# A hybrid decoder step on one core: wide state space tables, moved scans, value tiles and gate between the levels, the embedding's affine part on GpSimd

## The reference, cut to what matters

```python
x = layer_norm(concat(meta, prompt, sample), g_emb, b_emb)           # embedding norm
q, fpre, v, gate, u = split(x @ w_in + b_in)                         # five groups of 512
f = lb + (1 - lb) * sigmoid(fpre);  k = (1 - lb) * sigmoid(-fpre)
o, S = gated_linear_recurrence(q, k, v, f, S0)                       # 4 heads of 128 x 128
o_hg = o * rsqrt(mean(o * o)) * norm_g * silu(gate)
h[t] = a_bar * h[t-1] + B_bar @ u[t];  y = C @ h + d * u             # complex diagonal state space
z = gelu(y);  o_ssm = z * sigmoid(z @ w_glu + b_glu)
x1 = layer_norm(ALPHA * x + concat(o_hg, o_ssm) @ w_out, g1, b1)
s = scores of x1 against 2 x 8 x 128 keys; top 16 by top 16 -> 16 of 16384 experts per head
ffn = sum over experts of softmax weight * gelu(u_expert . x1) * v_expert
out = layer_norm(ALPHA * x1 + ffn, g2, b2)                           # also S and h at the end
```

## Time and profile before

| what | value |
|---|---|
| median of 3 runs | 1229.93 us (1229.81 to 1230.38) |
| profiled execution, its own time | 1228.41 us |
| its span, first to last instruction | 1226.6 us |
| mean granted TensorE clock | 0.982 |
| busy: PE, PEld | 1167.3 us (95%), 1103.2 us (90%) |
| busy: DVE, ACT, POOL | 778.3, 549.3, 848.5 us |
| read from HBM | 167.62 MB |

### The profile page before, as it was taken

How to read it: one execution, slowest core, us unless ns; L and a number is a source line. 1 busy time by engine, 2 the same in 40 slices (tenths; PEclk the granted TensorE clock), 3 DMA queues, 4 the chain that set the end, 5 groups by cost and what they waited for, 6 DMA issues and landing times.

```text
span 1226.6 us, 25373 instructions
## 1 busy us (share of the span) xinstructions
PE 1167.3 (95%) x8561; PEld 1103.2 (90%) x8561; DVE 778.3 (63%) x1645; ACT 549.3 (45%) x987; POOL 848.5 (69%) x745
## 2 busy tenths in 40 slices
PE   4999969989999999999999999989999999999995
PEld 3685767469899999999999999989999999999995
DVE  6908976339999999432899999953333333333336
ACT  2240132035576676776333333345554554554553
POOL 4991673056688988887555555578888888888884
PEclk9999978989999999999999999999999999999998
DMA  7331143243344445444333333344544544544442
GB/s 269 119 109 69 70 111 86 78 161 132 121 160 165 165 160 171 163 162 157 133 106 118 120 117 111 115 135 158 169 166 160 170 163 162 171 161 164 171 158 86
DMA packets 63623, 173.06 MB, mean 141 GB/s; under 512 B 9872, under 2 KB 19216, under 8 KB 63456
## 3 DMA queue, kind: packets, MB, share of 16 engines
q1 hardware_dynamic: 63584, 172.58, 42.1%
HBM read 167.62 MB, written 3.69 MB: 140 GB/s over the span
## 4 chain that ended last, share of the span: by engine, by line
PE 85%; DVE 9%; issue 2%; DMA 1%; SPq 1%; POOL 1%; ACT 0%; DVEq 0%; ACTq 0%; POOLq 0%
PE bank L835 33%; PE bank L738 25%; PE bank L808 13%; PE bank L794 5%; PE bank L521 3%; PE bank L712 2%; DVE q_dec L1263 2%; PE bank L694 1%; PE bank L756 1%; DVE pre L1276 1%; SPq L421 1%; DVE att L1229 1%; POOL s_samp L1614 1%; DMA w_ring<-in_w_in 1%; PE bank L563 1%
## 5 line engine op out<-in xcount | busy, mean ns | idle before, releaser
L1620 POOL TENSOR_TENSOR parts<-raw,parts 128x512 fp32r<-128x512 f32 x544 | 718.2, 1326 | 288.7 <-ACT parts L876 287.6
L876 ACT ACTIVATE parts<-raw 128x512 fp32r<-128x512 f32 x544 | 343.5, 632 | 456.9 <-PE bank L835 202.8
L835 PE MATMUL bank<-w_hi,parts 128*128 128x288 f32 x2048 | 407.6, 295 | 3.6 <-DVE w_lo L1477 2.4
L835 PEld LDWEIGHTS bank<-w_hi,parts 128*128 128x128 f32 x2048 | 327.7, 188 | 4.1 <-DVE w_lo L1477 2.6
L738 PE MATMUL bank<-xw,parts 128*128 128x288 f32 x2304 | 310.6, 296 | 2.1 <-DVE xw L1333 1.1
L738 PEld LDWEIGHTS bank<-xw,parts 128*128 128x128 f32 x2304 | 309.2, 189 | 3.2 <-issue 3.1
L835 PE MATMUL bank<-w_lo,parts 128*128 128x288 f32 x1024 | 301.5, 294 | 0.0
L1495 DVE TENSOR_TENSOR w_lo<-store,w_hi 128x288 fp32r<-128x288 f32 x122 | 147.7, 1211 | 241.5 <-ACT w_hi L1041 241.5
L835 PEld LDWEIGHTS bank<-w_lo,parts 128*128 128x128 f32 x1024 | 192.0, 188 | 0.0
L808 PE MATMUL bank<-xw,parts 128*128 128x288 f32 x1152 | 171.2, 300 | 0.0
L808 PEld LDWEIGHTS bank<-xw,parts 128*128 128x128 f32 x1152 | 156.1, 188 | 0.0
(11 more groups left out here) (295 smaller groups left out, 1027.3 us busy)
## 6 DMA issues: line engine op xcount, KB each, us to landing
raw<-in_blocks SPq DMA_DIRECT2D x272, 512.0 KB, 3.2
w_ring<-in_w_in SPq DMA_DIRECT2D x5, 2048.0 KB, 8.6
w_ring<-in_w_out SPq DMA_DIRECT2D x2, 2048.0 KB, 7.8
s_samp<-in_state SPq DMA_DIRECT2D x8, 256.0 KB, 5.9
rows_ln<-in_rows SPq DMA_DIRECT2D x4, 512.0 KB, 5.0
out_hg_sample<-s_samp SPq DMA_DIRECT2D x8, 256.0 KB, 5.1
rows_emb<-in_rows SPq DMA_DIRECT2D x2, 512.0 KB, 6.1
wglu<-in_w_glu SPq DMA_DIRECT2D x1, 1024.0 KB, 5.3
```

What stands on the lines that cost most here:

```text
L835: last = mm(v_bank(c)[:, 0:NP], vv, w[:, s, :], start=first and (a, w) == (0, w_hi), stop=False, skip_group_check=True)
L876: A(parts[:, q % 4, 0, :], raw[:, s % 4, (q % 2) * 512:(q % 2 + 1) * 512], ACT.Copy).then_inc(hi_ready, 1)
L1620: G.tensor_tensor(parts[:, q % 4, 1, :], raw[:, q // 2 % 4, (q % 2) * 512:(q % 2 + 1) * 512], parts[:, q % 4, 0, :].bitcast(F32), ALU.subt ...
```

## The change

It does these things, in the order of the kernel:

- The embedding norm's gain and shift leave the token tiles. VectorE makes mean and deviation of a tile, ScalarE normalizes it in one pass (`normalize`); gain and shift are put in while the transposed tile is read out of PSUM, per channel, half by ScalarE (`read_x`) and half by VectorE. The residual x, with gain and shift, is made later by GpSimd from the two rows, which are loaded behind z.
- SP's order: tokens, `ident`, the 16 columns `embt`, first weights, then the state space inputs and the rest; the third weight group before the moves of u; wglu waits for v instead of the gate; keysT behind the outputs.
- w1 and c_pow: first small powers of the pole (`pw`, `ck`), then each table by one wide complex product of 1024 elements per part, written straight into place. `rot` moves to VectorE: eight squarings, two tables of eight turns (`turns`), and one wide product of them.
- PE's order: w1's transposes, X, toep and then q. ScalarE applies the lower bound to f and k.
- v's token tiles and the gate move between the levels; the gate is projected by channel, in four groups, and multiplied into the transposed output (`oT`) by VectorE instead of into the token tiles.
- The last gelu of the late u blocks comes behind the first two `w_hi`; VectorE's eight additions for `x1_t` alternate with `w_lo`.
- The last two v blocks are done by halves of the channels, so that the first half's transposes and statistics come before the last products; `w_end` is a third buffer for it.

```diff
+        JOBS += [("w1T", b) for b in range(8)] + [("X", b) for b in range(6)] + [("toep", b) for b in range(4)]
         JOBS += [("q", m) for m in range(4)]
-        JOBS += [("w1T", b) for b in range(8)] + [("toep", b) for b in range(4)] + [("X", b) for b in range(6)]
-        JOBS += [("v", t) for t in range(3)]
...
-        BETWEEN = {h: job for h, job in zip(LEVELS, [("gate", t) for t in range(3)] + [("y", b) for b in range(3)])}
+        BETWEEN = {0: [("v", 0)], 1: [("v", 1)], 2: [("v", 2), ("gate", 0)], 4: [("gate", 1)], 8: [("gate", 2)],
+                   16: [("gate", 3), ("y", 0)], 32: [("y", 1)], 64: [("y", 2)]}
...
-            for i in range(2):
-                sp.dma_start(rows_emb[:, i, :], rows_in[i, :].partition_broadcast(P)).then_inc(rows_sem, 16)
...
-            sp.dma_start(cols[:, :], cols_in).then_inc(cols_sem, 16)
-            sp.dma_start(s5raw[:, :, :, :].rearrange("p a b c -> p (a b c)"), s5bc).then_inc(cols_sem, 16)
-            sp.dma_start(ident[:, :], consts_in[:, 0:P]).then_inc(consts_sem, 16)
-            sp.dma_start(iota[:, :], consts_in[:, P:2 * P]).then_inc(consts_sem, 16)
-            sp.dma_start(lane[:, :], consts_in[:, 2 * P:2 * P + 9]).then_inc(consts_sem, 16)
+            sp.dma_start(ident[:, :], consts_in[:, 0:P]).then_inc(ident_sem, 16)
+            sp.dma_start(embt[:, :], cols_in[:, NCOLS:NCOLS + 2 * DC]).then_inc(embt_sem, 16)
...
+            sp.dma_start(cols[:, :], cols_in[:, 0:NCOLS]).then_inc(cols_sem, 16)
+            sp.dma_start(s5raw[:, :, :, :].rearrange("p a b c -> p (a b c)"), s5bc).then_inc(cols_sem, 16)
+            load_w(1)
...
+            load_w(2)
...
-            for n in range(2, 7):
+            for n in range(3, 7):
                 load_w(n)
 
-            sp.wait_ge(gate_done, 3)
+            evacuated(sp, "v", 2)
...
+            sp.wait_ge(q_decayed, tiles_before(P) + 1)
+            sp.wait_ge(k_decayed, tiles_before(P) + 3)
+            for i in range(2):
+                sp.dma_start(rows_emb[:, i, :], rows_in[i, :].partition_broadcast(P)).then_inc(rows_sem, 16)
 
             computed(sp, "Sb", NB - 1)
-            sp.wait_ge(og_ready, 3)
-            sp.wait_ge(vm_ready, 9)
-            sp.dma_start(keysT[:, :, :], keys_t).then_inc(keys_sem, 16)
...
+            evacuated(sp, "oT", 2)
+            sp.wait_ge(vm_ready, 9)
+            sp.dma_start(keysT[:, :, :], keys_t).then_inc(keys_sem, 16)
...
+            last_product(0, 0)
+            last_product(1, 0)
+            last_product(0, 1)
+            y_transposes(0)
+            last_product(1, 1)
+            y_transposes(1)
...
+                A(pre[:, m, :], f_t[:, m, :], ACT.Identity, bias=lbv[:, 8 + m:9 + m], scale=lbv[:, 16 + m:17 + m])
+                A(k_t[:, m, :], k_t[:, m, :], ACT.Copy, scale=lbv[:, 16 + m:17 + m]).then_inc(f_pre, 1)
...
+            late_gelus(V_ROUND - 1, range(3))
...
+            late_gelus(V_ROUND - 1, [3])
...
+            w4 = [wide_tmp[:, k, :].rearrange("p (a j c) -> p a j c", j=SC, c=16) for k in range(2)]
+            braw = [s5raw[:, r, :, :].unsqueeze(2).broadcast_to([P, NPAIR, SC, 16]) for r in range(2)]
+            cc = [ck[:, r, :, :].unsqueeze(3).broadcast_to([P, NPAIR, SC, 16]) for r in range(2)]
...
+            link(product([(w1[h, 0, :, :, g, :], h) for g, h in enumerate((lower, upper))], braw, cc, ALU.subtract))
+            product([(w1[h, 1, :, :, g, :], h) for g, h in enumerate((lower, upper))], braw, cc[::-1],
+                    ALU.add).then_inc(w1_ready, 1)
...
+            base = (cs, sn)
+            for k in range(8):
+                square((squares[:, k, 0, :], squares[:, k, 1, :]), base)
+                base = (squares[:, k, 0, :], squares[:, k, 1, :])
...
+            link(product([(rot64[0], full)], coarse, fine, ALU.subtract))
+            link(product([(rot64[1], full)], coarse, fine[::-1], ALU.add))
+            cmul(V, link, [rot[:, r, :, 64:NCP] for r in range(2)], [turns[:, r, :, 0, 0:4] for r in range(2)],
+                 [wide(squares[:, 7, r, :], 4) for r in range(2)], small_tmp(4))
+            V.sem_inc(rot_ready, 1)
...
+                    last = V.scalar_tensor_tensor(gate[:, k, :], b[:, 0:NT], gcol[:, k:k + 1], gate_sig[:, k, :],
+                                                  ALU.add, ALU.mult)
...
+            dve.wait_ge(gate_done, HEADS)
+            for t, (t0, n) in enumerate(TILES):
+                computed(dve, "oT", t)
+                readout(V.tensor_tensor(ohg_t[:, :, t0:t0 + n],
+                                        bank_of("oT", t)[:, 0:4 * n].rearrange("p (h n) -> p h n", n=n),
+                                        gate[:, :, t0:t0 + n], ALU.mult), "oT", t)
...
+                    dve.wait_ge(x0_added, t + 1)
...
-                if c % 4 == 3:
-                    for s in range(2):
-                        dve.wait_ge(whi_ready, 2 * (c // 4) + s + 3)
-                        j = 2 * (c // 4) + s + 2
-                        V.tensor_tensor(w_lo[:, s, :], store[:, j, :], w_hi[:, s, :].bitcast(F32),
-                                        ALU.subtract).then_inc(wlo_ready, 1)
-            with V.Fori(3, NK // 2, 1) as i:
-                for s in range(2):
+                dve.wait_ge(whi_ready, c + 3)
+                V.tensor_tensor(w_lo[:, c % 2, :], store[:, c + 2, :], w_hi[:, c % 2, :].bitcast(F32),
+                                ALU.subtract).then_inc(wlo_ready, 1)
...
+            for r, (x, op) in enumerate(((c_in, ALU.add), (c_in[::-1], ALU.subtract))):
+                G.tensor_tensor(pool_tmp[:, 0, :, :, :], x[0], powers[0], ALU.mult)
+                link(G.tensor_tensor(pool_tmp[:, 1, :, :, :], x[1], powers[1], ALU.mult))
+                for g, h in halves:
+                    link(G.tensor_tensor(c_pow[h, r, :, 1:5, g, :], pool_tmp[h, 0, :, :, :],
+                                         pool_tmp[h, 1, :, :, :], op))
+            G.sem_inc(cpow_ready, 1)
+            link(G.memset(suf[:, :, :], 1.0))
...
+            pool.wait_ge(rows_sem, 32)
+            for t, (t0, n) in enumerate(TILES):
+                x = x_tok[:n, t, :]
+                link(G.tensor_tensor(x, x, rows_emb[:n, 0, :], ALU.mult))
+                G.tensor_tensor(x, x, rows_emb[:n, 1, :], ALU.add).then_inc(x0_added, 1)
```

More of the change, by code:

```diff
@@ L513, in weights, with project_part @@
                 return w_ring[:, n % 2, :, :]
+            def project_part(kind, m):
+                w = weights(W_GROUP[kind])
+                b = begin(kind, m)
+                for c in range(DC):
+                    last = mm(b[:, 0:NT], w[:, c, m * P:(m + 1) * P], x_t[:, c, :],
+                              start=c == 0, stop=c == DC - 1)
+                last.then_inc(ps_full, 1)
             def project(kind):
-                w = weights(W_GROUP[kind])
                 for m in range(4):
[L519 to L523, removed]
+                    project_part(kind, m)
             def project_tok(kind, t):
@@ L553, in _ @@
                 transposes(("w1T", b8), [(w1f[:, 4 * b8 + k, :], P) for k in range(4)])
+            pe.wait_ge(u4_moved, 16 * 16)
+            w1tf = w1_t[:, :, :, :].rearrange("p r a s -> p (r a) s")
+            for b6 in range(6):
+                b = begin("X", b6)
+                units = range(6 * b6, min(6 * b6 + 6, 32))
+                for k, un in enumerate(units):
+                    evacuated(pe, "w1T", un // 4)
+                    last = mm(b[:, k * NCH:(k + 1) * NCH], w1tf[:, un, :], u4[:, un % NPAIR, :],
+                              start=True, stop=True)
+                last.then_inc(ps_full, 1)
             pe.wait_ge(cpow_ready, 1)
@@ L566, in _ @@
                 last.then_inc(ps_full, 1)
[L570 to L577, removed]
-                    last = mm(b[:, k * NCH:(k + 1) * NCH], w1tf[:, un, :], u4[:, un % NPAIR, :],
-                              start=True, stop=True)
-                last.then_inc(ps_full, 1)
-            for t in range(3):
-                project_tok("v", t)
+            project("q")
             def levels(h):
@@ L846, in _, with last_product, y_transposes @@
                     v_block(i, s)
-            v_block(NK // 2 - 1, 0)
-            v_block(NK // 2 - 1, 1, final=True)
-            for h in range(2):
+            def last_product(s, h):
+                pe.wait_ge(wlo_ready, NK - 1 + s)
+                pe.wait_ge(lo_ready, 8 * ROUNDS - 3 + 2 * s + h)
+                hi, lo = (w_end[:, 0, :], w_end[:, 1, :]) if s else (w_hi[:, 0, :], w_lo[:, 0, :])
+                for c in range(4 * h, 4 * h + 4):
+                    for (a, w) in ((0, hi), (0, lo), (1, hi)):
+                        vv = parts[:, 2 * s + h, a, (c % 4) * P:(c % 4 + 1) * P]
+                        last = mm(v_bank(c)[:, 0:NP], vv, w, start=False, stop=False, skip_group_check=True)
+                    if s:
+                        last.then_inc(y_full, 1)
+            def y_transposes(h):
                 pe.wait_ge(yT_ready, 4 * (h + 1))
```

(38 more changed lines are left out.)

355 lines of the change are left out of this document (192 added, 163 removed).

## The result

The changed kernel took 1220.02 us (median of 4 runs, 1218.51 to 1220.39) against 1229.87 for the kernel before in the same set: ratio 0.9921, 95% interval 0.9908 to 0.9935. It is faster by 9.85 us; 7.5 were forecast. The profiled execution took 1219.73, its span is 1218.0 (before 1226.6, so 8.6 less).

A forecast was written before the change was run, and what follows sets the result against it. PE was taken as almost continuously busy from 257 us through the expert products, so gains lie ahead, near 800 and behind 1211. 3.2 + 3.7 + 0.6 = 7.5 us gave 1220.9 profiled, 1222.4 against the median; range 1215 to 1227.

The forecast's parts named there:

- The start: Kernel start to first projection: without the embedding rows PE starts at 17.0 instead of 21.9 us; gain 2 to 6.
- TensorE's queue: PE's work before the scan's result is needed: third weight group's 2.9 us wait goes, q ends at 87.1 us.
- the levels: Stage after the scan: VectorE enters at 94.6, PE becomes the longer, y complete at 152.0; gain over 20 us.
- w1: VectorE's table: small instructions to 28.4, wide ones 24.5 us at one pace with GpSimd (bounds 9.6, 26.8), ready at 53.0.
- rival (a): Wide table products on VectorE and GpSimd exclude each other: 28.4 us, w1 at 56.8, total 1226.2; chance 0.18.
- What is given back: Between y and GLU: SP's moves, late rows (171.7), GpSimd's residual (187.1) and scaling (9.0) put GLU at 196.9, leaving 4.0 us.
- Rival (c): Between y and GLU: GpSimd's residual is hidden, outputs set the end; GLU at 181, 1206.5 us in all; chance 0.08.
- Rival (d): GpSimd ahead of GLU: all fourteen instructions at their highest price beside VectorE, 40 instead of 24.4 us, total 1238; chance 0.05.
- The gate's product: Behind the GLU factors on VectorE: one more 128x512 pass on the path, 0.8 us lost, between 0.65 and 0.9.
- The handoff: Near 800 us between expert products: PE's waits of 2.4 and 1.3 us for w_lo go; gain 3.7, bounds 2 and 3.7.
- The tail: End of expert products: shorter statistics save 1.9 us, twelve transposes cost 1.3; net 0.6, bounds 0 and 1.9.
- the front: Everything up to the start of GLU, including the gate's product: 3.2 us gained.

The follow-up runs named there:

- the run with the swap: Changed kernel with GpSimd's six residual instructions behind the scaling of the eight states instead of ahead: 1213.72 us, 0.9881 of the kernel before.
- the tail undone: Changed kernel with only the edits behind 1195 us undone (blocks, w_low, transposes, half statistics): 1219.41 us, 0.9923 of the kernel before.
- the tables one after the other: Changed kernel with GpSimd's wide products for c_pow waiting until w1 is done: 1219.63 us, 0.9923 of the kernel before.
- the handoff undone: Changed kernel with only the gelu and x1_t addition orders near 800 us put back: 1224.94 us, 0.9962 of the kernel before.

## Why the prediction was right, step by step

- **The start, TensorE's queue, the levels**: right. First projection 16.96 (forecast 17.0), q's end 87.24 (87.1), VectorE's entry into the levels 94.72 (94.6), last y product 150.44 (150.7); y is complete at 151.0 (152.0).
- **w1**: at 52.7 where 53.0 was forecast, which is luck: two wrong steps cancel. The "some 33 small instructions of 0.17 us" were to end at 28.4 and ended at 37.1, held up by GpSimd; the eight wide ones, at 24.5, took 15.5, since GpSimd was done at 45.5. The one pace for both engines that the prediction took from the row was not what happened: they held each other up for whole instructions, the mechanism of rival (a), but this fell on the small instructions too, and its whole did not exceed the row's price. The experiment shows that w1 15 us earlier would have changed nothing; a later one was not tried.
- **What is given back**: rows landed at 171.45 (171.7), residual to 186.97 (187.1), scaling 8.1 (9.0), GLU at 195.91 (196.9; 195.9 to 197.0 in the four later runs that keep this order). Rival (c) fell for the reason given against it; the run with the swap shows what it would have been worth. Rival (d), 40 us for GpSimd's fourteen, measured 23.5.
- **The gate's product**: 0.65 us of wait, forecast 0.8.
- **The handoff**: 3.65 in the trace (forecast 3.7), 5.15 when undone. The step "bounds 2 and 3.7" was too narrow above, since it left the clock behind a wait out.
- **The tail**: forecast 0.6. No gain is shown: the 0.26 are those of the whole stretch from the first product of the v blocks on, and with the tail undone this stretch was 0.7 shorter still. The shorter statistics gave 1.2, the transposes took 1.2, and the last VectorE instruction took 0.6 more, a term that the forecast did not have.
- **Not forecast**: a lower clock in the 10 us behind 252 us, 0.77 of the second stage. The standing still ahead of GLU does not explain it: with the tables one after the other, the handoff undone and the tail undone TensorE stood still there for 11.9, 14.4 and 14.5 us, and the clock of the second 5 us was 1.00 as in the kernel before; with the residual behind the scaling it did not stand still, and the clock was 0.89. The cause is open. GLU itself was 1.05 shorter in this execution, but 11.1 to 11.5 in three of the four later ones, so no gain is read from it.
- **The sum**: the front gave 5.46 where 3.2 was forecast, 1.0 because GLU started earlier (196.9 was forecast), 1.05 from GLU's own length. So the sum of 7.5 is nearer to the 8.6 of span than its terms are, since the 0.77 takes some of this back.

What stays open is what share of the 9.85 us, beside 8.6 of span, is scatter between executions: the intervals reach from 8 to 11. The pieces of the front (the start, PE's order, the tables' form, the gate) were not undone one by one; their part is read from the trace of the change.

## What to carry to other kernels

When a front is shortened by 20 us and the end by 5, look in the chain for the in-order queues that now stand between: here two orders, on GpSimd and on ScalarE, and one more wait were worth some 19 us by the ratios, twice the change itself. A VectorE instruction with two operands in SBUF is priced by what GpSimd runs beside it, however small it is; put long GpSimd work that is wanted late behind the last such product, even if GpSimd idles until then. A wait on TensorE that lies on the path is counted with the matmuls behind it: of three that were removed or restored in these runs, 4.4, 3.9 and 3.65 us, each was worth 1.5 to 3.2 more. Off the path, with the residual still ahead of the scaling, the same 4.4 were worth nothing that can be measured.

## What the runs showed of the hardware that was not expected

An instruction of 128x16 took up to 2.4 us beside GpSimd's products (0.18 alone), a copy of 128x1088, with one operand, 2.40 (0.73 alone), and one product of 128x512 was held off for 7.33 through seven GpSimd instructions in a row. Which side pays changes: in the run with the residual behind the scaling the same squares met the same scaling, took 1.53, 0.70 and 0.70, and the scaling took 9.43 instead of 8.1. The clock fell to its lower level (0.50, 1.2 GHz) behind a wait of 2.4 us in one execution and stayed at 1.00 behind the same wait in another.
